# Moving operand of the upper feed-forward products read as two alternating halves

## The chip, the cores and the metric

The kernel runs on one core of a Trainium2 chip. The metric is the device time of one execution in microseconds (us). The kernel before takes 2439.66 us, the median of three runs (2433.91 to 2442.28).

## What is computed

The reference is a block of two transformer-like layers over 256 tokens of width 2048, all in fp32. The first layer has an RWKV-7 time mix with a multi-scale pooling beside it, the second a gated linear attention beside a sparse attention. Each ends in a feed-forward, and these two are what the change touches:

```python
# first layer
h2 = rms_norm(x, mlp_norm[i])                                   # 256 x 2048
x = x + jnp.square(jax.nn.relu(h2 @ w_ffn_up[i])) @ w_ffn_down[i]     # 2048 -> 8192 -> 2048
# second layer
m = rms_norm_2(h, ffn_norm_g)
return h + (jax.nn.silu(m @ w_gate) * (m @ w_up)) @ w_down      # 2048 -> 5632 (twice) -> 2048
```

Here the "upper" products are those from width 2048 up: `h2 @ w_ffn_up`, `m @ w_gate` and `m @ w_up`. The "lower" ones are those by `w_ffn_down` and `w_down`.

## The kernel before

**Split products.** TensorE multiplies operands of type fp32r, a rounded fp32, at a higher rate than plain fp32. To keep the precision, weights and tokens are each split in a high part (rounded to fp32r) and a low part (the rest), and a product is the sum of three: high by high, high weights by low tokens, low weights by high tokens. The helper `three` (line 621) issues these; all of them carry line 625. Products in plain fp32 stand at other lines, such as 715 at the start of the kernel, and appear in the profile without the ending `_r` on their operands.

**The upper products** are issued by `split_rows` (line 628) for one chunk of 512 weight columns at a time. The weights are stationary (128x128), the tokens are the moving operand: for each of 16 k-tiles 128 channels by 256 tokens. Four units `j` of a chunk are gone through in order; each has 2 column tiles `f` and 8 k-tiles `k`, with three products each. The result lies in PSUM as rows of channels by 256 tokens. The first feed-forward has 4 parts of 4 such chunks. The second has three parts with 3 groups of a gate chunk and an up chunk, and a last part with 2 groups. The gated linear attention uses `split_rows` too, with the tokens of norm "n4".

**The lower products** are issued by `split_tokens` (line 665). There the tokens are stationary and the weights are the moving operand, with 512 columns. They read other buffers (`XD`, `HD`, `actT`) than the upper ones.

**Where the tokens come from.** The table `TOK` (line 361) has for each norm the pair of buffers of high and low tokens: `HTH` and `HTL` for "n2", the norm ahead of the first feed-forward, `XH` and `HTL` for "n5", ahead of the second. Once the residual `xs` of four k-tiles is complete, TensorE turns it by transposes into PSUM (`turn`, line 650). ScalarE scales it by the gain and writes the high part (`tokens_high` at line 1388, the operation itself at line 1366). VectorE computes the low part as PSUM times gain minus high part (`tokens_low`, line 1882, operation at line 1890). The semaphores `x_high` and `x_low` count these. For the first chunk after a norm (`fresh`) TensorE waits for `x_low` as it goes along: the last transposes are issued after the first unit's first 24 products, and the last wait stands in unit 1 before k-tile 6 of column tile 0. Later chunks read the same token buffers again with no such wait.

**The weights** come by DMA on SyncE's queue into a ring of two slots. ScalarE makes each unit's high part (line 1366, 128x2048), VectorE subtracts it in place (line 1899, 128x2048), and `w_low` lets TensorE begin the unit. `w_used` hands the slot back.

**Order.** Each engine runs a program written out by hand. Within the feed-forwards TensorE waits for `w_low` of each unit, and at the start of a chunk for its PSUM banks, which VectorE or ScalarE empty.

Of the kernel before, what the change touches and what calls it, by code (L numbers as in the profile page):

```python
# [14 lines left out]
ALU = mybir.AluOpType  # L15
# [4 lines left out]
T = 256  # L20
TT = T // P
D = 2048
KT = D // P
# [98 lines left out]
def build(nc, inp, consts, out):  # L122
# [12 lines left out]
    def r32(ap, early=False):  # L135

        end = ap.offset + sum((n - 1) * step for step, n in list(ap.ap)[1:])
        known = places[ap.tensor.name]
        if ap.tensor.name == "arena":
            known = known[-EARLY:] if early else known[:-EARLY]  # L140
        for c, n, t in known:
            if c <= ap.offset and end < c + n:
                return bass.AP(tensor=t, offset=ap.offset - c, ap=[[n, P]] + [list(d) for d in ap.ap][1:])

    def high_of(ap, early=False):

        return r32(ap, early).bitcast(F32)
# [21 lines left out]
    PS = ctx.enter_context(nc.psum_tensor("PS", [P, 8, 512], F32))  # L169
# [3 lines left out]
    def con(name):  # L173
        at, n = CONST_AT[name]
        return cst[:, at:at + n]
# [13 lines left out]
    def area(at, *dims):  # L189
        n = int(np.prod(dims))  # L190
        assert at + n <= NA, (at, dims)
        return split(arena[:, at:at + n], dims)
# [5 lines left out]
    def along(ap, n):  # L198

        return ap.unsqueeze(len(ap.shape)).broadcast_to(list(ap.shape) + [n])  # L200

    ident, tri, eye64 = con("ident"), con("tri"), con("eye64")
    pair = [PS[:, 0:2, :], PS[:, 2:4, :]]

# [152 lines left out]
    ptok = area(AR_AT + 8192, TT, 256)  # L357
    pT = area(AR_AT + 8192, 2, T)
    fing = area(8240, 4, CW)

    TOK = {"n2": (HTH, HTL), "n3": (HTH, HTL), "n4": (XH, actT), "n5": (XH, HTL)}

# [62 lines left out]
    N_WAG, N_KRV, N_POOL, N_SMALL, N_OUT, N_F1, N_GATE = 0, 1, 7, 9, 10, 14, 46  # L425
    N_GLA, N_KCVC, N_KSVS, N_KWVW, N_GOQ, N_CMP, N_OUT2, N_REST2, N_F2, N_END = 50, 54, 55, 56, 57, 61, 62, 64, 66, 104
# [176 lines left out]
    def _(pe):  # L603
# [21 lines left out]
                mm = pe.matmul(dst, r32(w, early), r32(x, early), start=first and q == 0, stop=last and q == 2)  # L625
            return mm

        def split_rows(n, g, tokens, i=None, per=2, fresh=None):


            xh, xl = tokens
            for j in range(4):
                pe.wait_ge(S["w_low"], split_count(n, j, i, per))
                h, k0 = j // 2, j % 2 * 8
                if fresh and j < 2:
                    pe.wait_ge(S["x_low"], XSPLIT[fresh] + 4 + 2 * j)
                wh, wl = (a.rearrange("p (k n) -> p k n", k=8) for a in (high_home(n, i, j), unit_at(n % 2, j)))
                for f in range(2):
                    for k in range(8):
                        if fresh and j == 1 and f == 0 and k in (4, 6):  # L640
                            pe.wait_ge(S["x_low"], XSPLIT[fresh] + 5 + k // 2)
                        c = slice(f * P, (f + 1) * P)
                        mm = three(pair[g][:, f, h * T:(h + 1) * T], (wh[:, k, c], wl[:, k, c]),
                                   (xh[:, k0 + k, :], xl[:, k0 + k, :]), k0 + k == 0, k0 + k == KT - 1)
                    if f:
                        mm.then_inc(S["w_used"], 1)
                    if fresh and j == 0 and f == (fresh == "n4"):
                        turn(fresh, 3)
# [121 lines left out]
        for g in range(2 * (NCH - 1)):  # L770
            c, m0 = g // 2, g % 2 * 4
# [206 lines left out]
        for i in range(F1_PARTS):  # L978
            if i == F1_PARTS - 1:
                pe.wait_ge(S["ptok_loaded"], 32)  # L980
                for t in range(TT):
                    for k in range(2):
                        pe.transpose(PS[:, 4, k * T + t * P:k * T + (t + 1) * P], ptok[:, t, k * P:(k + 1) * P], ident)
                pe.transpose(PS[:, 5, 0:16], frow, ident[0:16, 0:16]).then_inc(S["side_turned"], 1)
            for c in range(4):
                if c < 2:
                    pe.wait_ge(S["sum_step"], i * 4 + (SUM["ffn1"] - 1 + c))
                else:
                    pe.wait_ge(S["ffn1_relu"], i * 4 + (c - 1))
                split_rows(N_F1 + c, c % 2, TOK["n2"], i, 8, fresh="n2" if i == c == 0 else None)  # L990
            for g in range(4):
                if g < 2:
                    pe.wait_ge(S["ffn1_relu"], i * 4 + (3 + g))
                else:
                    pe.wait_ge(S["sum_step"], i * 4 + (SUM["ffn1"] + g - 1))
                if i == F1_PARTS - 1 and g == 1:
                    pe.wait_ge(S["side_copied"], 1)
                    pe.wait_ge(S["rs_ready"], 1)
                split_tokens(N_F1 + 4 + g, pair[g % 2], lambda k: XD[:, k, :], lambda k: actT[:, k, :], i, 8,
                             ready=(lambda q: pe.wait_ge(S["ffn1_low"], i * 4 + (q + 1))) if g == 0 else None,  # L1000
                             after={0: lambda: turn("n3", g - 1)} if i == F1_PARTS - 1 and g else None)
# [22 lines left out]
        for c in range(4):  # L1024
            pe.wait_ge(S["sum_step"], SUM["gate"] + min(c + 3, 4))
            if c >= 2:
                pe.wait_ge(S["groups_read"], c + 3)
            split_rows(N_GLA + c, c % 2, TOK["n4"], fresh="n4" if c == 0 else None)
            if c == 0:
                factors_over_rows(1)  # L1030

# [275 lines left out]
        for c in range(4):  # L1307
            n = N_REST2 + c // 2
# [14 lines left out]
        def ffn2_part(n, groups, silus, sums, i=None, per=F2_N):  # L1323

            def at(v, step):
                return v if i is None else i * step + v

            units = UNITS[groups]
            for m in range(groups):
                if m == 0:  # L1330
                    pe.wait_ge(S["sum_step"], at(sums - 1, 4))
                else:
                    pe.wait_ge(S["ffn2_scaled"], at(silus + m, F2_GROUPS))
                split_rows(n + 2 * m, 0, TOK["n5"], i, per, fresh="n5" if i == m == 0 else None)
                if i == m == 0:
                    factors_over_rows(2)
                if m == 0:
                    pe.wait_ge(S["sum_step"], at(sums, 4))
                else:
                    pe.wait_ge(S["ffn2_mul"], at(silus + m, F2_GROUPS))  # L1340
                split_rows(n + 2 * m + 1, 1, TOK["n5"], i, per)
            for g in range(4):
                if g < 2:
                    pe.wait_ge(S["ffn2_scaled" if g == 0 else "ffn2_mul"], at(silus + groups, F2_GROUPS))
                else:
                    pe.wait_ge(S["sum_step"], at(sums + g - 1, 4))
                split_tokens(n + 2 * groups + g, pair[g % 2], lambda k: HD[:, k, :], lambda k: actT[:, k, :], i, per, units,
                             (lambda q: pe.wait_ge(S["ffn2_low"], at(silus + q + 1, F2_GROUPS))) if g == 0 else None)
# [7 lines left out]
    def _(act):  # L1356
# [8 lines left out]
        def copy(dst, src, scale=1.0):  # L1365
            return act.activation(dst, src, ACT.Copy, scale=scale)  # L1366
# [21 lines left out]
        def tokens_high(p, gain, c):  # L1388

            banks = 2 if p == "n4" else 4  # L1390
            for j in (2 * c, 2 * c + 1):
                act.wait_ge(S["norm_turned"], KT // 2 * NORMS[p] + j + 1)
                for q in range(2):
                    k = 2 * j + q
                    by = gain4[:, k:k + 1] if p == "n4" else col(gain, k)
                    ins = copy(r32(TOK[p][0][:, k, :]), PS[:, 8 - banks + j % banks, q * T:(q + 1) * T], by)
                ins.then_inc(S["x_high"], 1)

        def norm_chunk(p, gain, c):
# [16 lines left out]
        for j in range(1, KT // 2, 2):  # L1416
            act.wait_ge(S["norm_turned"], j + 1)
            for q in range(2):
                k = 2 * j + q
                ins = copy(actT[:, k, :], PS[:, j, q * T:(q + 1) * T], gain1[:, k:k + 1])  # L1420
# [78 lines left out]
        for g in range(2 * (NCH - 1)):  # L1499
            c, m0 = g // 2, g % 2 * 4  # L1500
# [345 lines left out]
    def _(v):  # L1846
# [35 lines left out]
        def tokens_low(p, gain, c):  # L1882
            banks = 2 if p == "n4" else 4
            th, tl = TOK[p]
            for j in (2 * c, 2 * c + 1):
                v.wait_ge(S["x_high"], XSPLIT[p] + j + 1)
                for q in range(2):
                    k = 2 * j + q
                    by = gain4[:, k:k + 1] if p == "n4" else col(gain, k)
                    ins = v.scalar_tensor_tensor(r32(tl[:, k, :]), PS[:, 8 - banks + j % banks, q * T:(q + 1) * T], by,  # L1890
                                                 high_of(th[:, k, :]), ALU.mult, ALU.subtract)
                ins.then_inc(S["x_low"], 1)

        def low(n, js, i=None, per=2, units=UNITS[4]):
# [869 lines left out]
```

## Time and profile before

| | |
|---|---|
| median of 3 runs | 2439.66 us (2433.91 to 2442.28) |
| the profiled execution's own time | 2437.74 us |
| its span, first to last instruction | 2435.6 us |
| mean granted clock of TensorE | 0.993 |
| busy: TensorE products, weight loads | 2395.8 us, 2194.3 us |
| busy: VectorE, ScalarE, GpSimd | 1358.3, 987.4, 191.5 us |
| DMA | 425.36 MB, mean 175 GB/s |

PE stands for TensorE's products, PEld for its weight loads, DVE for VectorE, ACT for ScalarE, POOL for GpSimd. Products on TensorE are pipelined: the next one starts before the last one ends, so their durations can't be added up, and the distance between starts is what one costs in a row of them. A few per cent of the products have no record.

### The profile page before, as it was taken

The page shows a single profiled execution, that of the slowest core. Times are in us where ns is not written, and L with a number is a line of the kernel's source. Part 1 is how long each engine was busy: PE and PEld are TensorE (multiplying, and loading weights), DVE is VectorE, ACT ScalarE, POOL GpSimd, SP SyncE. Part 2 cuts the span into 40 slices and gives each one's busy share as a digit, 9 for nine tenths or more (in the row PEclk, how much of TensorE's full clock was granted, in tenths as well). Part 3 has the DMA queues.
Part 4 walks back from the last instruction along what each step waited for, and adds up shares of the span by engine and source line. Part 5 has one row for each costly group of instructions (what it writes and reads, how often), then busy time and mean ns, then how long its engine had stood idle before and what let it go on. Part 6 is the DMA issues. An engine that isn't in the chain of part 4 may idle for free.

```text
span 2435.6 us, 39206 instructions
## 1 busy us (share of the span) xinstructions
PE 2395.8 (98%) x18076; PEld 2194.3 (90%) x18076; DVE 1358.3 (56%) x1134; ACT 987.4 (41%) x932; POOL 191.5 (8%) x139
## 2 busy tenths in 40 slices
PE   8998999999999999999999999999999999999999
PEld 7997888998998998988789999877998999999897
DVE  5597665544454444455457568575554554555553
ACT  4652244443333333344453364265433333433332
POOL 0003110020110110210000002000000000000000
PEclk9999999999999999999999999999999999999999
DMA  7553146665656656664556544244554754755644
GB/s 219 167 161 88 31 174 217 185 202 182 202 188 195 198 184 202 181 239 173 190 150 201 178 141 140 89 152 140 173 191 163 234 192 163 229 181 178 214 158 138
DMA packets 334528, 425.36 MB, mean 175 GB/s; under 512 B 4185, under 2 KB 249357, under 8 KB 333981
## 3 DMA queue, kind: packets, MB, share of 16 engines
q1 hardware_dynamic: 333053, 418.55, 53.2%
q0 software_dynamic: 1136, 4.17, 0.6%
q8 instruction: 142, 2.33, 0.4%
q10 hardware_dynamic: 176, 0.14, 0.0%
q14 instruction: 21, 0.17, 0.0%
HBM read 420.75 MB, written 2.10 MB: 174 GB/s over the span
## 4 chain that ended last, share of the span: by engine, by line
PE 90%; DVE 5%; issue 2%; ACT 2%; DMA 0%; POOLq 0%; POOL 0%; DVEq 0%; ACTq 0%
PE PS L625 81%; PE PS L824 1%; PE PS L715 1%; DVE ring_r L1941 1%; PE PS L661 1%; PE PS L1012 1%; PE PS L1292 0%; DVE ring_r L2249 0%; PE PS L1196 0%; ACT arena_r L1366 0%; DVE arena L2052 0%; PE PS L896 0%; PE PS L951 0%; PE PS L1120 0%; PE PS L943 0%
## 5 line engine op out<-in xcount | busy, mean ns | idle before, releaser
L625 PE MATMUL PS<-arena_r,arena_r 128*128 128x256 f32 (+1 forms) x6944 | 1544.2, 300 | 3.7 <-DVE ring_r L2249 1.4
L625 PEld LDWEIGHTS PS<-arena_r,arena_r 128*128 128x128 f32 x6944 | 1123.5, 188 | 60.2 <-issue 4.3
L1899 DVE TENSOR_TENSOR ring_r<-ring,arena_r 128x2048 fp32r<-128x2048 f32 x316 | 730.5, 2315 | 658.7 <-ACT arena_r L1366 658.7
L1366 ACT ACTIVATE arena_r<-ring 128x2048 fp32r<-128x2048 f32 (+1 forms) x394 | 691.6, 1761 | 977.0 <-PE PS L625 971.4
L625 PE MATMUL PS<-arena_r,ring_r 128*128 128x256 f32 x3072 | 852.3, 277 | 0.0
L625 PEld LDWEIGHTS PS<-arena_r,ring_r 128*128 128x128 f32 x3072 | 578.5, 188 | 0.0
L625 PE MATMUL PS<-ring_r,arena_r 128*128 128x512 f32 (+1 forms) x1504 | 539.0, 371 | 0.0
L625 PE MATMUL PS<-arena_r,actT_r 128*128 128x512 f32 (+1 forms) x1184 | 454.3, 384 | 0.0
L625 PEld LDWEIGHTS PS<-ring_r,arena_r 128*128 128x128 f32 x1504 | 275.8, 188 | 49.7 <-issue 1.4
L625 PEld LDWEIGHTS PS<-arena_r,actT_r 128*128 128x128 f32 x1184 | 222.3, 188 | 44.6
L625 PE MATMUL PS<-actT_r,arena_r 128*128 128x256 f32 (+1 forms) x656 | 184.5, 281 | 0.0
L625 PE MATMUL PS<-ring_r,actT_r 128*128 128x256 f32 x832 | 156.5, 290 | 6.6 <-DVE ring_r L1941 6.6
L625 PE MATMUL PS<-ring_r,ring_r 128*128 128x256 f32 x512 | 146.0, 285 | 0.0
L625 PEld LDWEIGHTS PS<-ring_r,actT_r 128*128 128x128 f32 x832 | 132.3, 196 | 9.3 <-DVE ring_r L1941 7.2
L625 PEld LDWEIGHTS PS<-actT_r,arena_r 128*128 128x128 f32 (+1 forms) x656 | 123.8, 189 | 0.0
L2249 DVE TENSOR_TENSOR ring_r<-ring,arena_r 128x1024 fp32r<-128x1024 f32 x56 | 72.6, 1313 | 60.0 <-ACT arena_r L1366 59.9
L625 PEld LDWEIGHTS PS<-ring_r,ring_r 128*128 128x128 f32 x512 | 99.3, 194 | 0.0
L1941 DVE TENSOR_TENSOR ring_r<-ring,actT_r 128x2048 fp32r<-128x2048 f32 x26 | 59.5, 2292 | 40.4 <-ACT actT_r L1366 40.2
L2692 POOL TENSOR_TENSOR arena_r<-arena 128x1024 fp32r<-128x1024 f32 x16 | 30.3, 1895 | 612.6 <-ACT arena L1605 612.6
L2733 POOL TENSOR_TENSOR arena_r<-arena,cst 128x1024 fp32r<-128x1024 f32 x9 | 23.0, 2552 | 690.0 <-DVE arena L2637 690.0
L1909 DVE SCALAR_TENSOR_TENSOR xs<-PS,small,xs 128x512 f32<-128x512 f32 x64 | 45.1, 747 | 40.1 <-PE PS L625 40.1
L1366 ACT ACTIVATE actT_r<-ring 128x2048 fp32r<-128x2048 f32 x26 | 49.8, 1920 | 42.9 <-PE PS L625 42.9
(339 smaller groups left out, 1403.6 us busy)
## 6 DMA issues: line engine op xcount, KB each, us to landing
ring<-in_w_ffn_up SPq DMA_DIRECT2D x32, 2048.0 KB, 10.3
ring<-in_w_ffn_down SPq DMA_DIRECT2D x32, 2048.0 KB, 8.1
ring<-in_w_in SPq DMA_DIRECT2D x22, 2048.0 KB, 8.3
ring<-in_w_gate SPq DMA_DIRECT2D x22, 2048.0 KB, 8.1
ring<-in_w_up SPq DMA_DIRECT2D x22, 2048.0 KB, 8.1
ring<-in_w_in SPq DMA_DIRECT2D x32, 1024.0 KB, 5.3
ring<-in_w_out SPq DMA_DIRECT2D x16, 2048.0 KB, 8.2
ring<-in_w_down SPq DMA_DIRECT2D x12, 2048.0 KB, 8.1
```

Source lines behind the costliest of these rows:

```text
L625: mm = pe.matmul(dst, r32(w, early), r32(x, early), start=first and q == 0, stop=last and q == 2)
L661: mm = pe.transpose(PS[:, 8 - banks + j % banks, q * T + t * P:q * T + (t + 1) * P], xs[:, t, k * P:(k + 1) * P], ident)
L715: mm = pe.matmul(half(0)[0:n, f, :], wag[:, k, f * P:f * P + n], actT[:, k, :], start=(k == 0), stop=(k == KT - 1))
L824: mm = pe.matmul(PS[h, bank, at:at + C], lhs(h, m, c, e), rhs(h, m, c, e), start=True, stop=True)
L1012: mm = pe.matmul(PS[:, 4 + t, :], pT[:, k, t * P:(t + 1) * P], pproj[:, c, k, :], start=(k == 0), stop=(k == 1))
L1366: return act.activation(dst, src, ACT.Copy, scale=scale)
L1899: v.tensor_tensor(r32(u), u, high_of(high_home(n, i, j)), ALU.subtract).then_inc(S["w_low"], counts(units, j))
L1909: ins = v.scalar_tensor_tensor(xs[:, t, at], pair[g][:, t], by[:, t:t + 1], xs[:, t, at], ALU.mult, ALU.add)
L1941: v.tensor_tensor(r32(w), w, high_of(high_at(u), True), ALU.subtract).then_inc(S["in_low"], 1)
L2249: v.tensor_tensor(r32(u), u, high_of(HIH[q % 4]), ALU.subtract).then_inc(S["w_low"], 1)
L2692: pool.tensor_tensor(r32(XD[:, 4 * c:4 * c + 4]), r, r, ALU.mult)
L2733: pool.tensor_tensor(r32(HD[:, 4 * m:4 * m + 4]), RQ[1], one, ALU.mult).then_inc(S["ffn2_high"], 1)
```

## The change

The 256 tokens of a k-tile are stored in another order, for the norms "n2" and "n5" alone. The word at position h*128 + i holds token 2i + h: even tokens in the first half of the 256 words, odd ones in the second. ScalarE and VectorE read PSUM in order and write to positions 0, 128, 1, 129, ... . VectorE reads the high part in that order too. TensorE reads the moving operand of the upper products in the same order, one word from each half in turn, so its result stands in PSUM in the order of the tokens as before. Norms "n3" and "n4", the transposes, the weights, the lower products, all semaphores and the order of instructions stay. The functions `unwoven` and `halves_of` are defined and not called.

```diff
+    def woven(ap):
+
+        return ap.rearrange("p (h i) -> p i h", h=2)
...
+    WOVEN = ("n2", "n5")
+
+    def laid(p, dst, src):
+
+        return (woven(dst), src.rearrange("p (i h) -> p i h", h=2)) if p in WOVEN else (dst, src)
...
-        def split_rows(n, g, tokens, i=None, per=2, fresh=None):
-
-
-            xh, xl = tokens
+        def split_rows(n, g, p, i=None, per=2, fresh=None):
+
+            view = woven if p in WOVEN else lambda a: a
+
+            xh, xl = TOK[p]
...
                         mm = three(pair[g][:, f, h * T:(h + 1) * T], (wh[:, k, c], wl[:, k, c]),
-                                   (xh[:, k0 + k, :], xl[:, k0 + k, :]), k0 + k == 0, k0 + k == KT - 1)
+                                   (view(xh[:, k0 + k, :]), view(xl[:, k0 + k, :])), k0 + k == 0, k0 + k == KT - 1)
...
-                    ins = copy(r32(TOK[p][0][:, k, :]), PS[:, 8 - banks + j % banks, q * T:(q + 1) * T], by)
+                    dst, src = laid(p, TOK[p][0][:, k, :], PS[:, 8 - banks + j % banks, q * T:(q + 1) * T])
+                    ins = copy(r32(dst), src, by)
...
-                    ins = v.scalar_tensor_tensor(r32(tl[:, k, :]), PS[:, 8 - banks + j % banks, q * T:(q + 1) * T], by,
-                                                 high_of(th[:, k, :]), ALU.mult, ALU.subtract)
+                    src = PS[:, 8 - banks + j % banks, q * T:(q + 1) * T]
+                    (dst, src), (high, _) = laid(p, tl[:, k, :], src), laid(p, th[:, k, :], src)
+                    ins = v.scalar_tensor_tensor(r32(dst), src, by, high_of(high), ALU.mult, ALU.subtract)
```

The calls of `split_rows` pass "n2", "n4" or "n5" in place of the pair of buffers.

## Rows read from the trace of the kernel before

**Rows 1.** Page: busy time, and the chain's shares by engine and line.
```profile
PE 2395.8 (98%) x18076; PEld 2194.3 (90%) x18076; DVE 1358.3 (56%) x1134; ACT 987.4 (41%) x932; POOL 191.5 (8%) x139
...
PE 90%; DVE 5%; issue 2%; ACT 2%; DMA 0%; POOLq 0%; POOL 0%; DVEq 0%; ACTq 0%
PE PS L625 81%; PE PS L824 1%; PE PS L715 1%; DVE ring_r L1941 1%; PE PS L661 1%; PE PS L1012 1%; PE PS L1292 0%; DVE ring_r L2249 0%; PE PS L1196 0%; ACT arena_r L1366 0%; DVE arena L2052 0%; PE PS L896 0%; PE PS L951 0%; PE PS L1120 0%; PE PS L943 0%
```

**Rows 2.** Chain in order of time: start us, us, what; over both feed-forwards.
```profile
446.28 520.19 PE PS L625 x3432
...
1712.72 19.19 PE PS L625 x168
...
1732.36 610.13 PE PS L625 x4512
...
2392.61 38.36 PE PS L625 x168
```

**Rows 3.** Groups by shape, 446 to 1150 us: the first feed-forward's upper products.
```profile
L625 PE MATMUL PS<-arena_r,arena_r 128*128 128x256 f32 x2032 | 346.7, 276 | 0.0
...
L625 PE MATMUL PS<-arena_r,ring_r 128*128 128x256 f32 x1016 | 280.7, 276 | 0.0
```

**Rows 4.** Instructions in order of time: start, us, engine, line; the first two of triples.
```profile
449.66 0.39 PE L625 MATMUL PS<-arena_r,arena_r 128*128 128x256 f32 x2
...
450.00 0.39 PE L625 MATMUL PS<-arena_r,arena_r 128*128 128x256 f32 x2
...
453.06 0.39 PE L625 MATMUL PS<-arena_r,arena_r 128*128 128x256 f32 x2
```

**Rows 5.** Chain in order of time: four other stretches of products.
```profile
14.87 6.91 PE PS L715 x32
...
112.46 22.94 PE PS L625 x192
...
445.41 0.87 PE PS L661 x8
...
1082.65 21.79 PE PS L625 x96
```

**Rows 6.** Groups and one line's instructions: ScalarE, VectorE and GpSimd by word.
```profile
L1366 ACT ACTIVATE arena_r<-ring 128x2048 fp32r<-128x2048 f32 x322 | 616.9, 1919 | 884.4 <-PE PS L625 878.7 <-DMA ring<-in_w_out 4.0 <-DMA ring<-in_w_in 1.6
L1366 ACT ACTIVATE arena_r<-ring 128x1024 fp32r<-128x1024 f32 x72 | 74.8, 1053 | 92.6 <-PE PS L625 92.6
...
L2725 POOL COPY arena<-arena 128x240 f32<-128x240 f32 x8 | 9.3, 1211 | 21.9 <-PE PS L1102 21.9
...
L2681 POOL TENSOR_SCALAR xs<-xs 128x240 f32<-128x240 f32 x8 | 6.5, 810 | 0.1
...
L1999 DVE COPY arena<-arena x1: 199/199/199, 145.3 to 145.3; 128x32 f32<-128x32 f32 x1
...
L2505 DVE TENSOR_TENSOR arena<-arena 128x8 f32<-128x8 f32 x6 | 1.0, 170 | 0.2
```

**Rows 7.** Groups, then order of time: the operations that make the tokens.
```profile
L1366 ACT ACTIVATE arena_r<-PS,pcol 128x256 fp32r<-128x256 f32 x48 | 18.8, 474 | 18.2 <-PE PS L661 18.2
...
L1890 DVE SCALAR_TENSOR_TENSOR arena_r<-PS,pcol,arena_r 128x256 fp32r<-128x256 f32 x48 | 19.9, 478 | 24.7 <-ACT arena_r L1366 24.7
...
446.76 1.66 DVE L1890 SCALAR_TENSOR_TENSOR arena_r<-PS,pcol,arena_r 128x256 fp32r<-128x256 f32 x4
...
1714.58 1.66 DVE L1890 SCALAR_TENSOR_TENSOR arena_r<-PS,pcol,arena_r 128x256 fp32r<-128x256 f32 x4
```

**Rows 8.** Stretches: us, busy by engine, granted clock of TensorE, DMA share, GB/s.
```profile
460.00:500.00 40.00, 40.00 (x356) 40.00 (x355) 18.32 (x9) 17.16 (x10) 11.61 (x4) 1.00 0.63 187
...
15.00:21.00 6.00, 6.00 (x30) 5.28 (x29) 3.38 (x7) 4.13 (x6) 0.00 (x0) 1.00 0.62 182
```

More of the change, by code:

```diff
@@ L200, in along, with unwoven, halves_of @@
         return ap.unsqueeze(len(ap.shape)).broadcast_to(list(ap.shape) + [n])
+    def woven(ap):
+        return ap.rearrange("p (h i) -> p i h", h=2)
+    def unwoven(ap):
+        return ap.rearrange("p (i h) -> p h i", h=2)
+    def halves_of(ap):
+        return ap.rearrange("p (h i) -> p h i", h=2)
     ident, tri, eye64 = con("ident"), con("tri"), con("eye64")
@@ L989, in _ @@
                     pe.wait_ge(S["ffn1_relu"], i * 4 + (c - 1))
-                split_rows(N_F1 + c, c % 2, TOK["n2"], i, 8, fresh="n2" if i == c == 0 else None)
+                split_rows(N_F1 + c, c % 2, "n2", i, 8, fresh="n2" if i == c == 0 else None)
             for g in range(4):
@@ L1027, in _ @@
                 pe.wait_ge(S["groups_read"], c + 3)
-            split_rows(N_GLA + c, c % 2, TOK["n4"], fresh="n4" if c == 0 else None)
+            split_rows(N_GLA + c, c % 2, "n4", fresh="n4" if c == 0 else None)
             if c == 0:
@@ L1333, in ffn2_part @@
                     pe.wait_ge(S["ffn2_scaled"], at(silus + m, F2_GROUPS))
-                split_rows(n + 2 * m, 0, TOK["n5"], i, per, fresh="n5" if i == m == 0 else None)
+                split_rows(n + 2 * m, 0, "n5", i, per, fresh="n5" if i == m == 0 else None)
                 if i == m == 0:
@@ L1340, in ffn2_part @@
                     pe.wait_ge(S["ffn2_mul"], at(silus + m, F2_GROUPS))
-                split_rows(n + 2 * m + 1, 1, TOK["n5"], i, per)
+                split_rows(n + 2 * m + 1, 1, "n5", i, per)
             for g in range(4):
```

## The prediction

> **What bounds the kernel now.** I read the page's busy shares and the shares of the chain of waits first: TensorE is busy for 98% of the span, and 81% of the chain is line 625, the one line that issues all split products [rows 1]. Then the chain in order of time over both feed-forwards: each is one unbroken piece of line 625, 520.19 us in the first and 610.13 us in the second, with no wait for another engine in it [rows 2]. So in the stages that the change touches nothing is hidden behind anything: what one of these products gains or loses is gained or lost at the end. Last the groups by shape and the instructions in order of time, to get the pace of one product. Its mean duration of 276 ns [rows 3] is not that pace, since products overlap; the starts are. Ten triples of products go from 449.66 to 453.06 us [rows 4], thirty products in 3.40 us: 113.3 ns each, with 256 columns, that is 2.26 columns a nanosecond.
>
> How many are there? The code issues 4 x 2 x 8 x 3 = 192 products for a chunk of 512 weight columns, and there are 16 chunks in the first feed-forward and 22 in the second (three parts of 6, one of 4): 38 x 192 = 7296. The trace has 2032 + 1016 = 3048 of the first one's 3072 between 446 and 1150 us [rows 3], the rest being lost records. A check on pace and count: the second feed-forward runs 718.3 us, from 1712.72 to 2430.97 [rows 2]. Its 4224 upper products at 113.3 ns are 478.7 us, its 1056 lower ones (3 parts of 4 x 72, and 4 x 48) at 227.0 ns (21.79 us for 96 [rows 5]) are 239.7 us, together 718.4. So 7296 x 113.3 ns = 827 us, a third of the kernel, are upper products.
>
> **The change part by part.** Nothing is added or removed in number: no instruction, DMA or wait more, and none moves in its queue. Three things change their access pattern.
>
> (a) TensorE's moving operand in 7296 products. Before, 256 consecutive fp32 words are read. After, the columns come from words 0, 128, 1, 129, ..., so that of two consecutive columns each lies 512 bytes from the other. PSUM is still written in order. The weights' side is untouched. The trace of before has no product whose moving operand is read like this, so its price has to be bounded.
> - From below: the operand is read as fast as before, or a little faster. What TensorE cannot beat is the pace of loading 128 weight columns: eight transposes with only 128 moving columns take 0.87 us [rows 5], 109 ns each. So the most that any reading order can give is 113.3 - 109 = 4.3 ns, or 7296 x 4.3 = 31 us.
> - Nearest known rate of TensorE below that: the plain fp32 products of line 715, with the same 256 columns, take 6.91 us for 32 [rows 5], 216 ns each, 1.19 columns a nanosecond. ScalarE goes through 1024 more words in 1919 - 1053 ns [rows 6], 1.18 a nanosecond. That is the highest rate shown here at which an engine need not have more than one fp32 word every time it reads. To hold 2.26 columns a nanosecond, TensorE must get two neighbouring words at once, and after the change no two neighbours in the order of reading are neighbours in memory. At 216 ns: 7296 x (216 - 113.3) = 749 us.
> - GpSimd is the one engine with a larger scattered read in this trace: the copy of line 2725 reads words 64 bytes apart, 1211 ns for 240, against 810 ns for 240 contiguous words of line 2681 [rows 6], a factor of 1.5. As a factor on 113.3 ns this is 170 ns a product, 7296 x 56.7 = 413 us.
> - From above: VectorE's copy of 32 words that lie 256 bytes apart takes 199 ns, its operations on 8 words 170 [rows 6], so at most 29 / 24 = 1.2 ns a word. If TensorE's scattered read were no faster than that, a product would take 309 ns, 7296 x 196 = 1428 us.
> I take 216 ns: it is a rate of TensorE itself, and with each word fetched alone there is no reason to be slower than the engine's own one-word rate. If the small tax that the contiguous read shows (113.3, not 109) doubled with it, it would be 226.7 ns, 827 us.
>
> Of this the Trainium skill has a rule that speaks against the change: Advanced Engine Details and Errata, "SBUF Cachelines", says that SBUF has lines of 16 bytes, that at least two accesses to a line are needed to hide the memory's latency, and that going to a different line with each access is penalised. It gives no size for the penalty. Read contiguously a line serves four columns, after the change one. No row of this trace shows TensorE doing that; the copy by GpSimd above agrees in sign, and the sum here does not use the rule.
>
> (b) ScalarE's writes of the high tokens, 32 operations of 128x256 of some 474 ns, and (c) VectorE's 32 for the low tokens, of 478 ns [rows 7], which write (and for the high part read) with the same 512-byte steps; their PSUM operand is read in order. I cost them at nothing. What hides them: after the last turn of n2 TensorE has 36 products, 4.1 us, until it waits for the last low tokens, at 446.28 + 4.1 = 450.4; VectorE ends them at 446.76 + 1.66 = 448.4 [rows 7]. For n5 it is 1712.72 + 4.1 = 1716.8 against 1714.58 + 1.66 = 1716.2, only 0.6 us of slack. If writing doubled the word part (some 0.25 us an operation, 4 + 4 in a row), n5 would be late by 1.4 us and n2 by nothing; with a slower TensorE the 36 products take 7.8 us and both are hidden again. So 0, at most 3 us.
>
> (d) Everything else has more room, not less: VectorE is busy 56% and ScalarE 41% [rows 1], weights come by DMA at a share of 0.6 of its engines [rows 8], all freed by the same semaphores as before. A slower TensorE only makes them wait. The clock: TensorE is granted 1.00, its 2.4 GHz level, in the upper products and also in the plain fp32 stretch at 216 ns [rows 8], so reading at the lower rate is no reason here for it to fall; I count nothing.
>
> The sum, against the profiled execution's own 2437.74 us (span 2435.6 and 2.1 around it): 2437.7 + 749 = 3186.7. The median of the three runs is 1.9 us above that execution; the forecast is **3187 us**.
>
> **Rivals.**
> 1. No change: the read side has room for one word per column wherever it lies, or the 512-byte step falls on another bank each time. For it speaks that VectorE and ScalarE show no clear cost of scattered words; against it that they ask for half of TensorE's rate or less. 2440 us, at most 3 above for (b) and (c).
> 2. Faster, the other side. The contiguous read is 4.3 ns a product over the weight-load pace, and where operands lie matters in this kernel: the same kind of product takes 22.94 us for 192, 119.5 ns, in the early projections with other places in SBUF [rows 5]. If that tax is two reads that meet in one part of the memory, and reading from two places in turn lets TensorE slip past it, all 7296 products fall to 109 ns: 2440 - 31 = 2409 us. It decides as soon as the scattered read costs nothing at all. Against it: the 512-column products pay the same 6% with half as much weight loading per column (227.0 against 2 x 113.3), so it looks like a property of the moving read itself, which the change makes harder.
> 3. Slower by a little: the read holds its rate but loses the good alignment, and the pace goes to the 119.5 ns of the early projections: 7296 x 6.2 = 45 us, 2485 us.
> 4. Slower, but by GpSimd's factor: 2440 + 413 = 2853 us; and by VectorE's upper bound, 3868 us.
>
> **How the numbers follow.** Half rate (3160 to 3290, from a pace of 212 to 230 ns): 0.62. No change: 0.13. Faster: 0.12. Slower by a little: 0.06. Rival 4: 0.07, half on each side of the forecast. Together: faster 0.12, same 0.13, slower 0.75, where "same" is within 0.3%, about what a measurement of this kernel can tell from no change (the three runs lie 0.34% apart). Cases of both signs are in play, so the range that holds 8 in 10 reaches over the gap: 2405 to 3290; the likeliest case has 3160 to 3290 for itself.
>
> **What would show it.** In the changed kernel's trace: the starts of consecutive upper products 216 ns apart in both feed-forwards, those of the lower products still 227 ns; the two stretches that the chain gives to line 625 longer by 7296 x 102.7 ns in all, 315 us in the first and 434 us in the second; longer idle time of VectorE and ScalarE before lines 1899 and 1366; granted clock 1.00; the operations of lines 1366 and 1890 at 128x256 still near 475 ns. The prediction is wrong if the starts stay at 113 to 120 ns (rivals 1 to 3), and its size is wrong if they lie at 170 or above 230.

## The result and the profile after

The changed kernel takes 2422.97 us, the median of 4 runs (2417.79 to 2423.44), against 2440.97 us for the kernel before beside it: a ratio of 0.9926, with a 95% interval of 0.9901 to 0.9951. Timed again in the last experiment it was 0.9953 (0.9939 to 0.9967). So it is faster by 0.5 to 0.7%, some 12 to 18 us, where I had forecast 749 us more. It lies within my range of 2405 to 3290 us, but only because that range was stretched over the gap to reach cases of the other sign; this speaks for nothing in the forecast. The profiled execution took 2423.44 us, its span is 2421.3 us.

The lines of the code are 18 to 22 further on: `three` is now line 643 (625 before), ScalarE's copy 1385 (1366), VectorE's operation on the low tokens 1912 (1890). First the page's busy shares and the chain:

```profile
PE 2383.4 (98%) x18076; PEld 2180.8 (90%) x18076; DVE 1362.9 (56%) x1134; ACT 992.1 (41%) x932; POOL 191.7 (8%) x139
...
PE PS L643 81%; PE PS L843 1%; PE PS L734 1%; DVE ring_r L1962 1%; PE PS L680 1%; PE PS L1031 1%; DVE ring_r L2270 1%; DMA arena<-in_w_in 1%; PE PS L1215 0%; PE PS L1191 0%; PE PS L1311 0%; ACT arena_r L1385 0%; PE PS L915 0%; DVE arena L2073 0%; PE PS L970 0%
```

The picture is that of [rows 1]: still TensorE for 98%, still one line. The chain of the changed kernel in order of time (start us, us, what):

```profile
448.32 515.78 PE PS L643 x3432
964.69 113.21 PE PS L643 x888
1078.78 21.78 PE PS L643 x96
1706.30 18.76 PE PS L643 x168
1725.51 603.27 PE PS L643 x4512
2378.27 38.36 PE PS L643 x168
```

The same products as in [rows 2], in pieces of the same counts, and each piece with upper products in it is shorter: 520.19 has become 515.78, 19.19 has become 18.76, 610.13 has become 603.27. The lower products are as they were: 96 of them take 21.78 us against 21.79 [rows 5], the last piece 38.36 as before. The pace of one upper product is seen in the instructions in order of time:

```profile
451.84 0.39 PE L643 MATMUL PS<-arena_r,arena_r 128*128 128x256 f32 x2
...
457.87 0.39 PE L643 MATMUL PS<-arena_r,arena_r 128*128 128x256 f32 x2
```

Eighteen triples, 54 products, in 6.03 us: 111.7 ns each, where [rows 4] had 113.3. Times 7296 that is 12 us. The granted clock is 1.00 as in [rows 8]:

```profile
460.00:500.00 40.00, 40.00 (x361) 40.00 (x360) 18.95 (x10) 16.04 (x10) 11.65 (x4) 1.00 0.66 196
```

And 361 products touch these 40 us instead of 356. What did get slower is the making of the tokens, ahead of the first feed-forward (its piece starts 2.0 us later here, 448.32 against 446.28, but these operations are not why: see the writes alone, below):

```profile
L1385 ACT ACTIVATE arena_r<-PS,pcol x16: 683/719/868, 382.2 to 449.4; 128x256 fp32r<-128x256 f32 x16
```

```profile
L1912 DVE SCALAR_TENSOR_TENSOR arena_r<-PS,pcol,arena_r x16: 653/686/791, 383.4 to 450.7; 128x256 fp32r<-128x256 f32 x16
```

Medians of 719 and 686 ns stand against means of 474 and 478 [rows 7].

### The profile page after: what moved, and what is told of

Same layout as the page of the kernel before. It is cut to its first block, busy times and chain, and to the rows that moved or that the text cites. A ratio compares the mean times of both kernels' runs of the same rounds, so it can differ in the third digit from the quotient of the medians.

```text
span 2421.3 us, 39206 instructions
## 1 busy us (share of the span) xinstructions
PE 2383.4 (98%) x18076; PEld 2180.8 (90%) x18076; DVE 1362.9 (56%) x1134; ACT 992.1 (41%) x932; POOL 191.7 (8%) x139
## 4 chain that ended last, share of the span: by engine, by line
PE 90%; DVE 5%; issue 2%; ACT 2%; DMA 1%; POOLq 0%; POOL 0%; SPq 0%; DVEq 0%; ACTq 0%
PE PS L643 81%; PE PS L843 1%; PE PS L734 1%; DVE ring_r L1962 1%; PE PS L680 1%; PE PS L1031 1%; DVE ring_r L2270 1%; DMA arena<-in_w_in 1%; PE PS L1215 0%; PE PS L1191 0%; PE PS L1311 0%; ACT arena_r L1385 0%; PE PS L915 0%; DVE arena L2073 0%; PE PS L970 0%
## 5 line engine op out<-in xcount | busy, mean ns | idle before, releaser
L643 PEld LDWEIGHTS PS<-arena_r,ring_r 128*128 128x128 f32 x3072 | 587.7, 191 | 0.0
```

## The experiments

In all of them the pace is read from the starts of products in order of time; a row of stretches gives the number of products that touch 17 us, one or two more than fit in.

**Reads alone, writes alone.** Where does the gain sit? The first kernel keeps `split_rows` as changed and lays the tokens down as before; the second does the reverse.

```diff
# e1_reads
-        return (woven(dst), src.rearrange("p (i h) -> p i h", h=2)) if p in WOVEN else (dst, src)
+        return dst, src
# e2_writes
-            view = woven if p in WOVEN else lambda a: a
+            view = lambda a: a
```

> TensorE reads the moving operand of both feed-forwards' upper products in the woven order, as in the changed kernel, but ScalarE and VectorE write the tokens contiguously, as before (so the columns of the upper products' results are in another order of tokens, nothing else differs). Theory A, the gain is in TensorE's read: the upper products start 111.7 ns apart, as in the changed kernel, against 113.3 before, 7296 x 1.6 = 12 us less than before, and token operations stay at 475 ns, so it is as fast as the changed kernel or up to 2 us faster. Theory B, the gain comes from where the stored words lie or from the timing of the writes: pace 113.3 ns and 2440 us.

> The other half alone: ScalarE and VectorE write the tokens of n2 and n5 in the woven order, TensorE reads the 256 words contiguously, as before (the results' columns are in another order of tokens). Theory A: pace 113.3 ns as before, token operations about 700 ns (ScalarE) and 670 ns (VectorE) as in the changed kernel against 475 before, of which 2 to 4 us reach the end: 2442 to 2446 us against 2441. Theory B: 111.7 ns and some 2425 us.

Reads alone: 0.9953 of before (0.9937 to 0.9968), as fast as the changed kernel. Writes alone: 1.0007 (0.9997 to 1.0017), no measurable difference. The chain of each:

```profile
445.67 515.77 PE PS L643 x3432
1729.96 603.27 PE PS L643 x4512
```

```profile
446.04 520.19 PE PS L643 x3432
1732.00 610.13 PE PS L643 x4512
```

The first has the changed kernel's pieces, the second those of before to 0.01 us. Theory A holds: the gain is in TensorE's read. The second kernel's token operations take 714 and 694 ns at the median, and nothing of this is seen at the end, where 2 to 4 us had been expected. The tightest place is ahead of the second feed-forward, where VectorE makes the last low tokens:

```profile
1714.22 2.19 DVE L1912 SCALAR_TENSOR_TENSOR arena_r<-PS,pcol,arena_r 128x256 fp32r<-128x256 f32 x4
```

The four operations together take 0.5 us longer (2.19 against 1.66 us [rows 7]), since each starts before the last one has ended. They end at 1716.4, and the product that needs the last of them starts at 1717.1, so 0.7 us are left.

**A sweep of reading orders, upper products.** A function gives the moving operand another order in each chunk of the first feed-forward, over the kernel before.

```diff
+    def turns(ap, h, j=1):
+        return ap if h == 1 else ap.rearrange("p (h i j) -> p i h j", h=h, j=j) if j > 1 else \
+            ap.rearrange("p (h i) -> p i h", h=h)
...
-                                   (xh[:, k0 + k, :], xl[:, k0 + k, :]), ...
+                                   (turns(xh[:, k0 + k, :], *mov), turns(xl[:, k0 + k, :], *mov)), ...
```

> The kernel before, with another reading order of the moving operand in each of the 16 chunks of the first feed-forward's upper products (the columns of their results are then in another order, some weights stand in another order too). In order of chunks: contiguous; then words from 2, 4, 8, 16, 32, 64 and 128 places in turn (512, 256, 128, 64, 32, 16 and 8 bytes apart); then 2 places with runs of 2, 4, 8 and 16 words; then contiguous with the 128 weight columns read at a step of 2 words; then 2 places with that; contiguous; 2 places. Theory A1, any turning between places hides the read's own tax: all patterns but contiguous ones at 111.7 ns. Theory A2, a new 16-byte stretch with each word costs unless two of them alternate: 2 places 111.7, 4 to 32 places far slower, up to 213 ns. Theory C, which was my forecast's reason (two neighbours must come together): refuted already for 2 places, would leave 128 places (8 bytes apart) fast and the others slow. Weights at a step of 2 words: 113.3 if loading has slack, more if the load reads pairs.

Medians in ns for 256 moving columns, by the number of places read in turn: contiguous 113, 2 places 112, 4 places 143, 8: 222, 16: 220, 32: 219, 64: 233, 128: 229. Two places with runs of 2, 4, 8, 16 words: 164, 127, 122, 122. With the weight columns at a step of 2 words the mean is 120.7 contiguous and 120.5 with 2 places. From the stretches (us, busy, products, clock, DMA share, GB/s), contiguous, 2, 4 and 8 places:

```profile
446.00:460.00 14.00, 14.00 (x125) 1.00 0.65 189
466.00:483.00 17.00, 17.00 (x154) 1.00 0.77 224
490.00:507.00 17.00, 17.00 (x122) 1.00 0.63 211
520.00:537.00 17.00, 17.00 (x78) 1.00 0.09 27
```

(the first is 14 us long). Theory A1 is refuted: turning is not free as such. A pace near my forecast's 216 to 227 ns is there from 8 places on, at a granted clock of 1.00. Two places are the exception, and A2 has the right shape, though not at 128 places, 8 bytes apart: there two words that share 16 bytes come one after the other, and the pace is as slow as with 8 places. Theory C, my forecast's reason, fails at both ends: 2 places should have been slow and 128 places (8 bytes apart) fast; they take 112 and 229 ns.

The weight columns at a step of 2 words, first contiguous, then with 2 places:

```profile
1097.00:1114.00 17.00, 17.00 (x144) 1.00 0.71 203
1119.00:1136.00 17.00, 17.00 (x143) 1.00 0.75 210
```

**The same for the lower products**, with 512 moving columns for each load of 128, so that loading weights cannot be what bounds them.

```diff
-                        mm = three(out[:, t, :], (xh(x)[:, tok], xl(x)[:, tok]), (wh[:, k, :], wl[:, k, :]), ...
+                        mm = three(out[:, t, :], (xh(x)[:, tok], xl(x)[:, tok]),
+                                   (turns(wh[:, k, :], *mov), turns(wl[:, k, :], *mov)), ...
```

> The same sweep on the first feed-forward's 16 lower chunks, whose moving operand is 512 weight columns and where one weight load of 128 columns stands against 512 moving ones (results' columns in another order). In order of chunks: contiguous; 2, 4, 8, 16, 32, 64, 128 and 256 places in turn (1024 down to 8 bytes apart); 2 places with runs of 2, 4 and 16 words; contiguous with the token columns of the load at a step of 2 words; 2 places with that; contiguous; 2 places. Theory A, the contiguous read has a tax of one part in 16 of its own: 227.0 ns contiguous, and 213 to 218 with 2 places, as loading does not bound these. Theory D, the tax is a meeting of the weight load's and the moving read, which the new order evades in the upper products: with loading active half the time here, 2 places give at most half of it back, 220 or more, or nothing.

Means in ns: contiguous 226.8; 2 places 215.8; 4: 283; 8: 487; 16: 435; 32: 433; 64: 431; 128: 461; 256: 453. Two places with runs of 2, 4, 16 words: 333, 250, 240. The load at a step of 2 words: 233.2 contiguous, 216.8 with 2 places. Contiguous, then 2, 4 and 8 places, then a step of 2 words (256 places):

```profile
529.00:546.00 17.00, 17.00 (x77) 1.00 0.65 239
550.00:567.00 17.00, 17.00 (x80) 1.00 0.70 245
572.00:589.00 17.00, 17.00 (x61) 1.00 0.55 179
600.00:617.00 17.00, 17.00 (x36) 1.00 0.28 91
...
990.00:1007.00 17.00, 17.00 (x39) 1.00 0.26 101
```

Theory A has the numbers and D does not: with half as many loads for each moving column the whole 11 ns of 227 goes, where D allowed half of it at most. So the contiguous fp32r read has a tax of about 5% here, the same per column with twice the loads (2 x 113.3 against 226.8). (Loads were not "active half the time": by their records they fill 14.08 of the 17.00 us of the first stretch, some 186 ns each. What is halved is their number. No run reads contiguously with no loads beside it.) This also tells what bounds the upper products now. The moving read alone would allow some 215.8 / 2 = 107.9 ns, an estimate; they run at 111.7, and making the load slower (the step of 2 words) moves them to 120.5 while the lower ones with 2 places stay within 1 ns. So the changed kernel's upper products are bound by loading weights.

**How far apart?** Within stretches of 2d words the order is 0, d, 1, d+1, ...

```diff
+    def near(ap, d):
+        return ap if d == 0 else turns(ap, 2) if 2 * d == ap.shape[1] else ap.rearrange("p (b h i) -> p b i h", h=2, i=d)
```

> The kernel before, with the moving operand (512 weight columns) of the first feed-forward's 16 lower chunks read from two places in turn at different distances d: within each stretch of 2d words the order is 0, d, 1, d+1 and so on (the results' columns are in another order). In order of chunks: contiguous, d = 2, 4, 8, 16, 32, 64, 128, 256 words, contiguous, d = 128, 64, 16, contiguous, d = 256, 128. Theory E, it is enough that a word's neighbour is read two words later, wherever the other place is: 216 ns at every d. Theory F, the two places must lie in different parts of the memory: 216 at d = 256 (seen) and at some multiples, near 430 ns at others, above all at small d. Theory G, the turn is free only if a long run follows from each place: the pace grows as d falls, since each stretch of 2d words begins anew, 227 or more at d below 32.

d = 2 takes 226.7 ns, like contiguous; d = 4, 8, 16, 32, 64, 128 and 256 all take 215.8. Contiguous, d = 2, d = 4:

```profile
533.00:550.00 17.00, 17.00 (x77) 1.00 0.63 233
554.00:571.00 17.00, 17.00 (x77) 1.00 0.68 245
575.00:592.00 17.00, 17.00 (x80) 1.00 0.74 229
```

None of the three theories has it: beyond d = 2 neither distance nor length of run matters for two places. At 2 words apart nothing is gained, at 4 words, 16 bytes, all of it (3 words was not run). The Trainium skill's page Advanced Engine Details and Errata, "SBUF Cachelines", gives SBUF lines of 16 bytes; the step between d = 2 and d = 4 agrees with this size.

**What is counted?** Theory I was formed from these numbers and put to the test on new orders.

```diff
+        "2 step 2": lambda a: a.rearrange("p (h i s) -> p s i h", h=2, s=2),
+        "2 step 4": lambda a: a.rearrange("p (h i s) -> p s i h", h=2, s=4),
+        "4 by 4": lambda a: a.rearrange("p (b h i) -> p b i h", h=4, i=4),
+        "far line": lambda a: a.rearrange("p (h j) -> p h j", h=128).rearrange("p (a b) j -> p b a j", a=64),
```

> Again the 512 moving columns of the first feed-forward's 16 lower chunks, one reading order each (columns of the results in another order). Theory I, taken from the two sweeps before: TensorE takes words in pairs of reading positions, the even and the odd ones each through a reader of its own, and what costs is how often a reader's next word lies in another stretch of 16 bytes: 1 in 4 of its words 216 ns, 1 in 2 227 ns, each one 283 to 460. In order of chunks: contiguous (1 in 2, 227); 2 places (1 in 4, 216); 2 places, within each a step of 2 words (1 in 2, 227); the same at a step of 4 and of 8 words (each word, over 283); 4 places 4 words apart within 16 words, and 16 words apart within 64 (each word in turn between two stretches, 283 as with 4 far places); 8 places 4 words apart (over 430); a step of 2 words (each, about 452); 2 places with runs of 4 words (1 in 2: 227, though 16 such runs took 240 and 4 took 250); every second stretch of 16 bytes, then the others (1 in 2, 227). Then 2 places at a step of 2, contiguous, contiguous, 2 places, contiguous. Theory J, turning between two places is itself what helps, whatever the step: 216 at steps 2, 4 and 8 too.

Measured: 2 places at a step of 2 words 227.0, at 4 words 453, at 8 words 461; 4 places 4 words apart 268, 16 words apart 269; 8 places 480; step 2 453; two places with runs of 4 words 250; every second stretch 231. In stretches: 2 places; the same at a step of 2; at a step of 4; 4 places 4 words apart; every second 16-byte stretch:

```profile
551.00:568.00 17.00, 17.00 (x80) 1.00 0.71 246
572.00:589.00 17.00, 17.00 (x76) 1.00 0.69 226
600.00:617.00 17.00, 17.00 (x39) 1.00 0.15 40
...
770.00:787.00 17.00, 17.00 (x65) 1.00 0.60 218
...
1022.00:1039.00 17.00, 17.00 (x75) 1.00 0.70 229
```

Theory J is refuted: turning between two places at a step of 2 words gains nothing and at 4 words runs at half rate. Theory I has the fast cases: 216 where each of the two alternating positions stays in its 16 bytes for 4 of its words, 227 where for 2, more where each word is in another. It misses by 4 for every second stretch (231 for 227) and by 23 for runs of 4 at two far places (250 for 227), though it counts these like the contiguous order. And where each word is in another stretch it gives only a span, within which the runs lie far apart: 4 places 268 to 283, two places with runs of 2 words 333, a step of 2 words 453, 8 places 480 to 487. In the first two each of the positions goes back and forth between two stretches before it leaves them, in the last two it does not; whether this is the difference was not tested. So the count orders the cases up to 227 ns and not the slower ones, and that there are two readers is a model which fits them, not something a trace shows.

**Using it further.** Two kernels build on the changed one. In the first the weights of the output projection and of both feed-forwards' lower products are read from two places as well, and VectorE puts the columns in order as it adds. The second does so in the gate and second output projections too, and lays down the input projection's tokens woven.

```diff
# in both: the lower products' moving operand, and VectorE's addition to the residual
+                        ... (look(wh[:, k, :]), look(wl[:, k, :])),        # look = woven
+                x, y = x.rearrange("p (h i) -> p h i", h=2), y.rearrange("p (i h) -> p h i", h=2)
# in the second besides, for example
+                                   (woven(XH1[j % 2][:, k, :]), woven(XL1[j % 2][:, k, :])), ...
```

> The changed kernel, and besides the 512 weight columns of the output projection's, both feed-forwards' lower products read from two places in turn; VectorE undoes the order of the columns as it reads PSUM and adds to the residual, so the result is right. Products with 512 moving columns: 384 + 1536 + 1056 = 2976. At 216 against 227 to 229 ns, 11 to 13 ns each: 33 to 38 us less than the changed kernel, 2385 to 2392 us, if VectorE's additions stay hidden (theory A). If its reads of PSUM at a step of 2 words take 1.5 times as long (as its writes did in the changed kernel) the last addition of each chunk is later by 0.3 to 0.6 us, hidden but in the chunks with a turn and at the end: 2 to 5 us of it back.

> The kernel of the run before this, and besides the gate projection's and the second output projection's weights (384 + 384 products with 512 moving columns) and the input projection's tokens (1536 products with 256) read from two places in turn, the tokens laid down by ScalarE and VectorE so, the weights' order undone as PSUM is read; the result is right. Theory A: the gate's and second projection's pace from 231 to 236 down to 216 to 218, 768 x 16 = 12 us; the input projection's from 119.5 to 111.7, 1536 x 7.8 = 12 us, less 2 to 4 us for the slower writing of the first tokens: 18 to 22 us below the run before. Theory H, pace 119.5 there is not the same tax but that of the operands' places in memory, which turning does not remove: 8 to 12 us.

The first takes 2389.61 us, a ratio of 0.9805 (0.9789 to 0.9821), within what was expected. VectorE's reads of PSUM at a step of 2 words cost nothing: its 64 additions in the feed-forwards take 746 ns on the average, as against 747 before.

```profile
L1933 DVE SCALAR_TENSOR_TENSOR xs<-PS,small,xs 128x512 f32<-128x512 f32 x64 | 45.1, 746 | 32.7 <-PE PS L643 32.7
```

The second takes 2380.25 us, 0.9764 (0.9746 to 0.9781), 58 us below the kernel before and the fastest here. The two medians are 9.4 us apart; the spans of the two profiled executions, 2388.0 and 2373.6 us, are 14.4 apart, but the second one's is the shortest of its four. Either is less than the 18 to 22 expected, and 9.4 alone would suit theory H (8 to 12); the pace in the trace decides between the theories. The second kernel's chain:

```profile
24.44 3.91 ACT ring_r L1390 x2
28.38 8.15 DVE ring_r L1977 x4
39.04 44.74 PE PS L647 x384
87.43 21.64 PE PS L647 x192
...
1136.63 5.18 PE PS L647 x24
```

192 products of the input projection take 21.64 us where [rows 5] has 22.94. The same 17 us of that projection, before and in the second kernel:

```profile
91.70:108.70 17.00, 17.00 (x145) 1.00 0.59 187
```

```profile
91.70:108.70 17.00, 17.00 (x155) 1.00 0.61 187
```

From start to start it was 117.8 or 120.0 ns before, by the buffer that is read, and is 111.7 now for all. So turning removes this excess too, and theory H falls. That it is the same tax is not shown: at the feed-forwards the contiguous read takes 113.3, and why it takes 4 to 7 ns more here stays open. The stretch from the first product to the output projection is 8.0 us shorter, but its first product starts 3.5 us later (39.04 against 35.55), behind ScalarE and VectorE that write the first tokens woven with nothing to cover them. The gate and second output projections gave 5.8 and 4.0 us, 9.8 together for the 12 expected; 24 products of the gate projection now take 5.18 us, 216 ns each, as expected.

**The changed kernel again.**

> The changed kernel once more, for a narrower interval. From its own trace: 7296 upper products at 111.7 against 113.3 ns are 12 us, and the first products of chunks that took 115 to 127 ns before give some 2 us more; 14 us, a ratio of 0.994, is what the mechanism explains. A ratio below 0.992 would ask for another gain besides.

0.9953 (0.9939 to 0.9967), which is 11.5 us by the median of before, with 8 to 15 in the interval: the 14 of the mechanism lie inside, and no other gain is needed. The first comparison's 18 us are a difference of medians. Its profiled executions differ by 14.3, of which 13.2 are in the five pieces of the chain over the feed-forwards (1302.6 against 1289.4 us); the other 1.1 is what remains of stages that both kernels have alike.

## Why the prediction was wrong

- *What bounds the kernel*: right. TensorE's pace in the upper products went to the end in full; 113.3 ns, the count of 7296 and the share of the kernel stand. Two readings beside it are off. No record is lost in either feed-forward: the 24 products missing from 3072 run before 446 us, where the window begins, and the trace has all 3072 and 4224. And [rows 2] has only part of each feed-forward in its long piece, 3432 of 4608 products and 4512 of 5280.
- *(a), the step that failed*: "To hold 2.26 columns a nanosecond, TensorE must get two neighbouring words at once", and from this the choice of 216 ns out of 109 to 309. No row had shown that, and the runs refute it: the upper products take 111.7 ns with two places in turn, no neighbours together, and 229 with 128 places. What the sweeps put in its place: two places at least 16 bytes apart are cheaper than the contiguous order, 215.8 against 226.8 ns where loads don't bind. A count of how often even and odd reading positions each go to another 16 bytes (half as often with two places) fits this; it is a model, and it doesn't size the slower orders. The price I gave, 216 to 227 ns, is near that of another access, 219 to 233 ns for 8 or more places; it came from plain fp32 products and ScalarE, so that is luck rather than the reason confirmed. I had taken "scattered" for one thing, and two places are not eight.
- *The lower bound*, 109 ns, came from transposes in plain fp32. Loading the fp32r weights allows 111.7, so the gain in pace was 12 us and not 31.
- *(b) and (c)*: 0 with at most 3 us, right: 1.0007 (0.9997 to 1.0017) for the writes alone. The size of one operation was guessed well where it was taken as a risk (0.2 us more for the 0.25 assumed), but the sign to look for, "still near 475 ns", was wrong: 719 and 686. The cover is larger than I counted: 24 products of the first unit and 18 of the next, 42 and not 36, come before the last wait. And four operations in a row grew by 0.5 us together, so n5 was not late at all.
- *(d)*: right, clock included: 1.00 at every pace of the sweeps.
- *Rival 2*, with a chance of 0.12, has the sign and the place of the gain, the contiguous read's tax, at too high a price (31 us). Its mechanism, two reads that meet in one part of the memory, is not borne out: the gain is the same from 4 to 256 words apart, and it is whole with half the loads. The argument that I held against it, that the 512-column products pay the same 6%, was a right observation read backwards: a tax of the moving read itself is what the change could remove. In the 512-column products all of it went; in the upper ones 1.6 ns, down to the pace of loading. *Rival 3* fails: the pace stayed below 113.3 ns, and the woven order took the early projections' 119.5 to 111.7 as well.
- *What would show it*: the starts at 111.7 ns told at once that of my cases only rival 2's sign was left. The Trainium skill's rule on SBUF's lines (Advanced Engine Details and Errata, "SBUF Cachelines"), weighed beside (a), speaks of a penalty for a different line with each access. Here each access does go to a different line than the one before it, and there is none; at a step of 2 words every line is hit twice in a row and the rate is half. On both counts these measurements decide against the rule as it is put, while the 16 bytes agree.

## What to carry to other kernels

Where TensorE streams an fp32r moving operand, read it from two places at least 16 bytes apart, one word from each in turn and each place contiguous: about 5% off a product of 512 columns, which loading weights does not bind, and 1.5% (113.3 to 111.7) off one of 256, which it comes to bind. Put the order right where VectorE empties PSUM, which cost nothing here, or where the operand is written under cover. Before giving a price to an unfamiliar access pattern, list the neighbouring patterns (2, 4, 8 places) and ask which of them the rows really speak of. A pace that stays the same per column whether there are few loads beside it or many, as 113.3 and 226.8 ns did, is worth a test of the read itself.

## What the runs showed of the hardware

- An fp32r moving operand read contiguously takes 226.8 ns for 512 columns in the feed-forwards (231 in the gate projection, 216 with two places); two places in turn 215.8, four 268 to 283, eight or more 431 to 487. A step of 2 words (8 bytes) within contiguous memory already halves the rate (453).
- Weights of 128 columns at a step of 2 words load more slowly: 120.5 ns a product against 111.7. They also slow a contiguous moving read (226.8 to 233.2) but hardly one from two places (216.8, against 215.8 to 216.7 without the step). So a contiguous read's cost does depend on the load beside it; how is open.
- ScalarE writing 128x256 words to two places in turn, and VectorE writing and reading one operand so, take about 700 ns against 475. VectorE reading PSUM at a step of 2 words takes no longer (746 against 747 ns for 128x512).
